# Moving twenty blocks of modulation sums from the first weighted sum to the two query stages

## The reference, cut to what matters

```python
def adaln(cvec, w, b):                      # w: 1024 x 6144, one per layer
    m = jax.nn.silu(cvec) @ w + b           # two conditioning vectors: context and latent
    return jnp.split(m[:, None, :], 6, axis=-1)
for l in range(2):
    h = modulate(rms_norm(x, g_mix[l]), m[0], m[1])
    x = x + m[2] * mixer[l](h)
    h = modulate(rms_norm(x, g_ffn[l]), m[3], m[4])
    x = x + m[5] * peer(h, w_q[l], keys[l], u[l], v[l])
y = rms_norm(x, final_g)
def peer(h, w_q, sub_keys, u_tab, v_tab):
    q = h @ w_q                             # 8 heads x 2 halves x 128
    s = q . sub_keys                        # 128 keys for each head and half
    ...                                     # top 16 of each half, top 16 of the pairs, softmax g
    return sum_k g_k * gelu(h . u_tab[i_k]) * v_tab[i_k]
```

## Time and profile before

| | |
|---|---|
| Time, median of 3 runs | 2504.21 us (2499.90 to 2505.34) |
| The profiled execution's own time | 2514.36 us |
| Its span, first to last instruction | 2512.6 us |
| Mean granted TensorE clock | 0.963 |
| PE busy | 2295.6 us (91% of the span) |
| DVE busy | 1727.8 us (69%) |
| ACT busy | 912.1 us (36%) |
| POOL busy | 1162.9 us (46%) |
| DMA | 771.15 MB, 307 GB/s over the span |

### The profile page before, as it was taken

How to read it: one execution, slowest core, us unless ns; L and a number is a source line. 1 busy time by engine, 2 the same in 40 slices (tenths; PEclk the granted TensorE clock), 3 DMA queues, 4 the chain that set the end, 5 groups by cost and what they waited for, 6 DMA issues and landing times.

```text
span 2512.6 us, 38357 instructions
## 1 busy us (share of the span) xinstructions
PE 2295.6 (91%) x11829; PEld 1699.1 (68%) x11829; DVE 1727.8 (69%) x3913; ACT 912.1 (36%) x1695; POOL 1162.9 (46%) x673
## 2 busy tenths in 40 slices
PE   6797999999877999999989889999999999999998
PEld 3686999999874343343458479999999944444443
DVE  7986798888555666676748747998885344455555
ACT  3344446666542111111044444666665510000002
POOL 2623587777773222222229444777777821111110
PEclk9898999999998999999999899999999999999999
DMA  8423378999999999999933023679999999999994
GB/s 304 160 96 123 114 223 313 381 386 376 399 418 408 404 399 408 400 409 409 387 125 109 0 84 118 200 269 377 386 378 380 407 398 393 383 374 395 398 397 188
DMA packets 195778, 771.15 MB, mean 307 GB/s; under 512 B 21728, under 2 KB 22880, under 8 KB 160224
## 3 DMA queue, kind: packets, MB, share of 16 engines
q1 hardware_dynamic: 120512, 402.81, 43.0%
q0 software_dynamic: 36864, 268.45, 27.1%
q10 hardware_dynamic: 38304, 98.71, 10.1%
HBM read 701.08 MB, written 68.81 MB: 306 GB/s over the span
## 4 chain that ended last, share of the span: by engine, by line
PE 53%; DMA 20%; DVE 15%; POOL 5%; issue 5%; ACT 2%; SPq 0%; ACTq 0%; DVEq 0%; POOLq 0%
PE ps L1790 24%; DMA raw<-in_v 12%; PE ps L1553 7%; PE ps L1554 7%; PE ps L1555 7%; PE ps L1772 4%; DMA raw<-in_u 4%; POOL w_lo L603 4%; DVE ga L1088 2%; DVE ps L1289 2%; DVE ps L1370 1%; DVE work L1372 1%; PE ps L1725 1%; DMA uv_stat<-in_uv,picked 1%; ACT w_hi L729 1%
## 5 line engine op out<-in xcount | busy, mean ns | idle before, releaser
L603 POOL TENSOR_TENSOR w_lo<-raw,w_hi 128x1024 fp32r<-128x1024 f32 x330 | 796.8, 2421 | 512.8 <-ACT w_hi L729 511.5
L1790 PE MATMUL ps<-raw,work 128*128 128x512 f32 x2048 | 909.7, 605 | 63.7 <-DMA raw<-in_v 47.2
L1553 PE MATMUL ps<-h_hi,w_hi 128*128 128x256 f32 (+1 forms) x2560 | 776.9, 303 | 49.3 <-POOL w_lo L603 48.6
L1790 PEld LDWEIGHTS ps<-raw,work 128*128 128x128 f32 x2048 | 392.7, 194 | 579.4 <-issue 535.3
L1554 PE MATMUL ps<-h_lo,w_hi 128*128 128x256 f32 (+1 forms) x2560 | 756.5, 295 | 0.0
L1555 PE MATMUL ps<-h_hi,w_lo 128*128 128x256 f32 (+1 forms) x2560 | 756.1, 295 | 0.0
L1553 PEld LDWEIGHTS ps<-h_hi,w_hi 128*128 128x128 f32 x2560 | 494.3, 193 | 63.4 <-POOL w_lo L603 60.3
L1554 PEld LDWEIGHTS ps<-h_lo,w_hi 128*128 128x128 f32 x2560 | 495.0, 193 | 0.0
L1555 PEld LDWEIGHTS ps<-h_hi,w_lo 128*128 128x128 f32 x2560 | 493.9, 193 | 0.0
L729 ACT ACTIVATE w_hi<-raw 128x1024 fp32r<-128x1024 f32 x330 | 347.7, 1056 | 137.1 <-DMA raw<-in_u 64.7
L977 ACT ACTIVATE wgt<-dots (+1 forms) x256 | 53.1, 207 | 712.0 <-DVE uv_stat L1431 213.3
(11 more groups left out here) (201 smaller groups left out, 2521.7 us busy)
## 6 DMA issues: line engine op xcount, KB each, us to landing
raw<-in_u SPq DMA_DIRECT2D x256, 512.0 KB, 6.7
raw<-in_v SPq DMA_DIRECT2D x256, 512.0 KB, 8.7
a_dram<-ga ACTq DMA_DIRECT2D x128, 256.0 KB
g_dram<-work ACTq DMA_DIRECT2D x16, 2048.0 KB, 12.1
work<-a_dram ACTq DMA_DIRECT2D x120, 256.0 KB, 8.5
work<-in_mod_w SPq DMA_DIRECT2D x56, 512.0 KB, 10.3
hots<-in_mod_w SPq DMA_DIRECT2D x32, 512.0 KB, 3.6
raw<-in_wq SPq DMA_DIRECT2D x32, 512.0 KB, 3.5
```

The source lines that it names most:

```text
L603: nc.gpsimd.tensor_tensor(w_lo[:, m % RING, :], raw[:, m % RING, :], w_hi[:, m % RING, :].bitcast(F32), ALU.subtract).then_inc(lo_ready, 1)
L1553: mm(out, w_hi[:, s, cols], h_hi[:, k, first:], start=n == 0, stop=False)
L1790: last = mm(ps[:, Y_DENSE[NT - ND_TILES + t] + half, :], wf[:, b, t * P:(t + 1) * P], raw[:, s, half * 512:(half + 1) * 512], start=first, ...
```

## The change

Blocks 32 to 43 are summed in the query stage of layer 0 and blocks 80 to 87 in that of layer 1; the first weighted sum keeps 36 blocks, in nine rounds: three in the first turn, as before, and two in each later turn (`OTHER_TURN`: the first and the third eighth). In each query stage six blocks come before the first group of `top_keys`, and two after each group until there are no more (12 = 6 + 2 + 2 + 2, 8 = 6 + 2). Since `keys` takes the place of `c_all`, the conditioning rows are copied once to DRAM (`c_dram`) and read to `uv_work` (`c_rows`) ahead of each query stage. SP issues these transfers and the loads of the moved blocks between those of `wq`. The product of each sum, which nobody reads, goes to the place of `wf`.

```diff
-MOD_ROUNDS = (SUM_BLOCKS - MOD_EARLY) // MSLOTS
+QUERY_MODS = (range(MOD_EARLY, MOD_EARLY + 12), range(SUM_BLOCKS - KC, SUM_BLOCKS))
+QUERY_FIRST, QUERY_EACH = 6, 2
+QUERY_AT = (4, 5, 6, 7, 8, 9, 12, 13)
+SWEEP_MODS = range(QUERY_MODS[0].stop, QUERY_MODS[1].start)
+MOD_ROUNDS = len(SWEEP_MODS) // MSLOTS
+OTHER_TURN = {0: 1, 2: 2}
...
+        c_rows = uv_work.rearrange("p (g d) -> p g d", g=2)
+        unread_q = wf[:, :, :].rearrange("p a t -> p (a t)").bitcast(BF16).rearrange("p (g d) -> p g d", g=2)
...
+            sp.wait_ge(c_ready, 3)
+            sp.dma_start(c_dram[:, :], c_all.rearrange("p g d -> p (g d)")).then_inc(c_stored, 16)
+            sp.wait_ge(proj_taken, R0["out"] + 1)
+            sp.wait_ge(c_stored, 16)
+            sp.dma_start(uv_work, c_dram[:, :]).then_inc(c_rows_loaded, 16)
...
             for layer in range(DEPTH):
+                blocks = QUERY_MODS[layer]
+                if layer:
+                    sp.wait_ge(rows_used, SLOTS)
+                    sp.dma_start(uv_work, c_dram[:, :]).then_inc(c_rows_loaded, 16)
                 stream(f"wq{layer}", 0, RING, RING)
                 if layer == 0:
                     sp.wait_ge(mod_summed, 2 * MOD_EARLY)
                     sp.dma_start(keys[:, :, :], io["keys"][0]).then_inc(keys_loaded, 16)
-                stream(f"wq{layer}", RING, HS - RING, 4)
+                else:
+                    sp.wait_ge(conv_done, KC - CONV_DVE)
+                for n in blocks[:MSLOTS]:
+                    mod_load(n)
+                for m in range(RING, HS):
+                    stream(f"wq{layer}", m, 1, 1)
+                    if m in QUERY_AT[:len(blocks) - MSLOTS]:
+                        mod_load(blocks[MSLOTS + QUERY_AT.index(m)])
...
-                            sp.dma_start(mod_late[:, k, :],
-                                         one(io["mod_w"], i * (TURN // 8 * MSLOTS) + (MOD_EARLY + j // 8 * MSLOTS + k))
+                            block, k = SWEEP_MODS.start + mods[j // 8] * MSLOTS, j % 8 // 2
+                            sp.wait_ge(mod_summed, i * (4 * MSLOTS) + 2 * (block + k + 1))
+                            sp.dma_start(mod_late[:, k, :], one(io["mod_w"], i * (2 * MSLOTS) + (block + MSLOTS + k))
                                          ).then_inc(mod_raw[k], 16)
                 if layer == 0:
-                    turn(0, False, range(1, 4))
+                    turn(0, False, {1: 0, 2: 1, 3: 2})
                     with sp.Fori(1, TURNS - 1) as i:
-                        turn(i, False, range(4))
-                    turn(TURNS - 1, True, range(MOD_ROUNDS - 4 * (TURNS - 1)))
+                        turn(i, False, OTHER_TURN)
+                    turn(TURNS - 1, True, {0: OTHER_TURN[0]})
...
-                nc.vector.tensor_tensor_reduce(unread[:, g, :], ring[:, k, :],
-                                               c_all[:, g, :] if g or first is None else first, 1.0, 0.0,
+                nc.vector.tensor_tensor_reduce(out[:, g, :], ring[:, k, :],
+                                               rows[:, g, :] if g or first is None else first, 1.0, 0.0,
                                                ALU.mult, ALU.add, accum_out=sums[:, k, g:g + 1]).then_inc(mod_summed, 1)
...
+                blocks = QUERY_MODS[layer]
+                def query_sums(first, count):
+                    for n in blocks[first:first + count]:
+                        for g in range(2):
+                            mod_group(0, 0, n // MSLOTS * MSLOTS, n % MSLOTS, g, rows=c_rows, out=unread_q)
+                        if n % MSLOTS == MSLOTS - 1:
+                            mod_bias(0, 0, n // MSLOTS * MSLOTS)
+                dve.wait_ge(c_rows_loaded, 16 * (layer + 1))
+                query_sums(0, QUERY_FIRST)
                 for q in range(HS // 4):
                     dve.wait_ge(s_taken, layer * HS + 4 * (q + 1))
                     each = [(t, c) for t in range(NT) for c in range(4 * q, 4 * q + 4)]
@@ -1392,6 +1431,8 @@
                     for t, c in each:
                         last = nc.vector.max_index(key_u[:, t, c, 8:16], vals[:, t, c, 8:16], s_all[:, t, c, :])
                     settle(last)
+                    query_sums(QUERY_FIRST + q * QUERY_EACH, QUERY_EACH)
+                dve.wait_ge(mod_ready, blocks.stop // MSLOTS)
...
-                            block = MOD_EARLY - MSLOTS + j // 8 * MSLOTS
-                            mod_group(i, TURN // 8 * MSLOTS, block, j % 8 // 2, j % 2, mod_late)
+                            block = SWEEP_MODS.start + mods[j // 8] * MSLOTS
+                            mod_group(i, 2 * MSLOTS, block, j % 8 // 2, j % 2, mod_late)
```

More of the change, by code:

```diff
@@ L354, in build @@
         mod_summed = sem("mod_summed")
+        c_stored = sem("c_stored")
+        c_rows_loaded = sem("c_rows_loaded")
         mod_ready = sem("mod_ready")
@@ L425, in build @@
         out_stored = sem("out_stored")
+        c_dram = nc.dram_tensor("c_dram", (P, 2 * D), F32)
         a_dram = nc.dram_tensor("a_dram", (N_KEYS // 2, P, 2 * ND), F32).ap()
@@ L487, in mod_load_late @@
             def mod_load_late(k):
-                sp.dma_start(mod_late[:, k, :], one(io["mod_w"], MOD_EARLY + k)).then_inc(mod_raw[k], 16)
+                sp.dma_start(mod_late[:, k, :], one(io["mod_w"], SWEEP_MODS[k])).then_inc(mod_raw[k], 16)
             for dst, src in ((x[:, :, :], io["x"]), (mod_b[:, :], io["mod_b"]), (gains[:, :, :], io["gains"]),
@@ L545, in _ @@
                     sp.wait_ge(s_done, HS)
+                    sp.wait_ge(mod_summed, 2 * SWEEP_MODS.start)
                     conditioning()
@@ L580, in _ @@
                 if layer == 0:
-                    sp.wait_ge(mod_summed, 2 * SUM_BLOCKS)
+                    sp.wait_ge(mod_summed, 2 * SWEEP_MODS.stop)
                     sp.dma_start(keys[:, :, :], io["keys"][1]).then_inc(keys_loaded, 16)
@@ L789, in gated @@
                 m0 = M0[name]
-                act.wait_ge(mod_ready, [MOD_EARLY - 2 * KC, SUM_BLOCKS][layer] // MSLOTS)
+                act.wait_ge(mod_ready, [MOD_EARLY - 2 * KC, SWEEP_MODS.stop][layer] // MSLOTS)
                 with act.Fori(0, 2) as i:
@@ L1077, in _, with mod_group @@
             dve.wait_ge(first_loaded, 5 * 16)
-            def mod_group(i, step, block, k, g, ring=mod_w, first=None):
+            def mod_group(i, step, block, k, g, ring=mod_w, first=None, rows=c_all, out=unread):
                 if k == 0 and g == 0:
@@ L1484, in turn @@
                                     dve.wait_ge(a_stored[s], 16 * (N_KEYS // 4))
-                            block = MOD_EARLY - MSLOTS + j // 8 * MSLOTS
-                            mod_group(i, TURN // 8 * MSLOTS, block, j % 8 // 2, j % 2, mod_late)
+                            block = SWEEP_MODS.start + mods[j // 8] * MSLOTS
+                            mod_group(i, 2 * MSLOTS, block, j % 8 // 2, j % 2, mod_late)
                             if j % 8 == 7:
-                                mod_bias(i, TURN // 8 * MSLOTS, block)
+                                mod_bias(i, 2 * MSLOTS, block)
                         if final and layer == 0 and j == SPAN + 8:
@@ L1493, in sweep @@
                 if layer == 0:
-                    turn(0, False, range(1, 4))
+                    turn(0, False, {1: 0, 2: 1, 3: 2})
                     with dve.Fori(1, TURNS - 1) as i:
-                        turn(i, False, range(4))
-                    turn(TURNS - 1, True, range(MOD_ROUNDS + 1 - 4 * (TURNS - 1)))
+                        turn(i, False, OTHER_TURN)
+                    turn(TURNS - 1, True, OTHER_TURN)
                 else:
@@ L1502, in sweep @@
                 if layer == 0:
-                    dve.wait_ge(mod_ready, SUM_BLOCKS // MSLOTS)
+                    dve.wait_ge(mod_ready, SWEEP_MODS.stop // MSLOTS)
                     at = (6 + 2) * KC
```

2 lines of the change are left out of this document (removed).

## The result

The change made the kernel slower: 2537.26 us median of 4 runs (2534.46 to 2540.77) against 2504.78 us of the kernel before in the same session, a ratio of 1.0125 with a 95% interval of 1.0102 to 1.0148. The direction was forecast, the size was not: 2513 us was predicted, with 2531 us as the upper end.

A forecast was written before the change was run, and what follows sets the result against it. It took memory transfers to bound the weighted sums and VectorE the selection. A gain of 21 us, delays of 26 us (layer 0) and 4 us (layer 1) gave +9 us on 2504.2: 2513 us, range 2492 to 2531 us.

The forecast's parts named there:

- What bounds the kernel: First weighted sum: TensorE waits for blocks of `v` on a full memory path; at the selection, VectorE's lateness delays TensorE one for one.
- The gain of 21 us, from 15 to 26: First weighted sum: twenty blocks fewer to load there save 21 us, with 15 and 26 as ends.
- The bound from the second sum: First weighted sum: turns 2 to 4 gain at least 14.8 us, since the second sum's need 352.5 us.
- Its sign of being wrong: First weighted sum: a length over 490 us would show that the forecast gain was wrong.
- The delay in layer 0, 26 us: Layer 0's query stage: GpSimd's low parts stretch the moved sums, making VectorE 26 us late at the selection, from 19 to 29.
- The low clock behind the wait: Layer 0's selection: after an idle time of 25 us or more, the lower clock adds 2 us, 0 to 5.
- The copy at nothing: Start of layer 0's query stage: copying conditioning rows delays `wq` some 6 us, covered by waits; 3 us kept for upper end.
- Layer 1, 4 us: Layer 1's query stage: eight moved blocks cost 4 us, from 0 to 9, part of the delay being caught up.
- The sum: Whole kernel: -21 + 26 + 4 = +9 us, a median of 2513 us; ends -9 and +29.
- The sums fit the waits: Query stages, both layers: VectorE stays on time and only the gain is left, 2483 us; chance 1 in 10.
- The gain isn't there: First weighted sum: single-load landing time sets the waits, gain under 8 us, total 2526 us or more; chance 1 in 12.
- SP is the one that is late: Query stage: `wq` loads behind waits for sums make TensorE later than VectorE, to 2530 us; chance under 1 in 20.

## Why the prediction was wrong in size

By its own steps:

- **What bounds the kernel.** Right for the selection: VectorE's last instruction of it and TensorE were both 33.9 us late. Half right for the weighted sum. TensorE does wait for blocks of `v` while the DMA share is near 1, but the waits that cost time stand at fixed blocks of each span of 16, where gate pieces, `mod_w` and `v` are issued together. The position of these waits was in the trace before.
- **The gain of 21 us, from 15 to 26.** This is the step that failed. It took a turn as one pool of bytes, at 1.29 us a block. The change took its rounds from the stretches of eight blocks where loads were few and kept them in those where they are many, so 3 to 8 us came. With the rounds apart turns 2 to 4 took 348.0 us instead of 366.9 in one profile, 18.9 us less, but the timed run that left the blocks out shows 14 us (10 to 18) for both steps together. So the place of the rounds is the larger part of what was missing; why even then less than 21 us came isn't shown. The bound from the second sum, 14.8 us at the least, was no bound, since that stage has its own placing and its waits fall elsewhere; it also rested on the longest of fourteen profiles of that stage. Its sign of being wrong, a first sum of over 490 us, was too lax: 489.6 us did not raise it.
- **The delay in layer 0, 26 us.** The mechanism and the count were right. From their real start at 229.90, 4.2 us behind the 225.7 of the count, the first group came at 259.19 (count: 255.0), the fourth stretch of sums at 318.60 (315.1) and the copy at 346.76 (342.5). Less the 4.2 us, the count was off by 0.1 us at the end. With the whole 2.40 us for each low part it would have come some 3 us later than it did. It was wrong to take 26 instead of the 28 that it gave, and wrong that 2 us come back at the selection: the instruction at 428.85 took 2.44 us as before. TensorE's wait grew by 28.0 us. The low clock behind the wait, counted as up to 5 us more, was no difference: 0.50 for the first 5 us, and also 0.50 in the second profile of before, behind a wait of 4.7 us (0.71 in the first).
- **The copy at nothing.** Nearly right: it cost 1.6 to 1.9 us, inside the 3 us kept for the upper end. The rest of the 4.2 us by which the first sum started late was there ahead of the copy, and in the kernel before, profiled again, as well.
- **Layer 1, 4 us.** Right: against the first scores the selection came 3.7 us later, which is what the wait has grown by (7.9 - 4.2). The 3.8 us of L1404 did come back, as forecast (it took 0.56 us), those of L1412 did not.
- **The sum.** -21 + 26 + 4 + 0 = +9 was forecast. Between the second profile of before and the profile after it reads: +2.3 us up to the first scores, +29.0 from there to the selection, -6.3 in the first weighted sum and +3.8 in layer 1's query stage, +28.8 in all, where the two executions differ by 28.9; four other differences of 2.2 to 2.5 us cancel. The medians differ by 32.5 us, so 4 us remain that the profiles don't assign. Of the 24 us between 2513 and 2537, 13 to 18 are the missing gain, 3 the delay and 2 the copy.
- **The rivals.** "The sums fit the waits" is refuted for this layout, but is what happens when the second input is in PSUM. "The gain isn't there", at 2526 us or more, came nearest and had 1 in 12. Its reason, the time that a single load needs whatever stands beside it, isn't what the runs show: the same loads in other places brought 6.5 to 8 us. "SP is the one that is late" didn't come: TensorE's wait ended with VectorE's selection.

## What to carry to other kernels

A saving in bytes is worth what it takes off the place where the consumer waits: before pricing it as a mean rate, find the blocks at which the waits stand and see whether the loads that leave are those issued just ahead of them. An instruction put in another engine's idle time is priced by what runs beside it there, not by its length where it stood: 24 sums took 53.6 us beside GpSimd's low parts and 27.8 us when these couldn't hold them up. One input in PSUM in place of SBUF, for half of the sums, made the difference between 0.9992 and 0.9933 here, with the same work at the same place. And before a start that is 4 us late is put down to the change, the kernel before is to be profiled twice: 2.6 of these us were its own.

## What the runs showed of the hardware

- A `tensor_tensor_reduce` of 128 x 1024 with its second input in PSUM took 1.21 to 1.22 us in all 24 cases in the query stage of layer 0, where GpSimd makes its low parts; with both inputs in SBUF it took 2.29 us on average there, and 3.4 us when held up. The hold-up was 2.2 us, less than the 2.40 us that a low part lasts. Even an addition of 128 x 8, of 0.17 us, took 2.24 us.
- A wait of 3.84 us for a block was followed by a granted clock of 0.53 for 5 us and of 0.79 for the next 5. Behind a wait of 2.38 us it stayed at 1.00. Of the 7 us by which turn 2 differed between the two forms 4.8 us were slower matmuls.
- Twenty 512 KB loads less lowered the DMA rate of the stage from 390 to 375 GB/s and its time by 6 to 8 us of 498. With the loads that stayed in other places it was 476.6 us.
